# Index scores in column groups, and seven block products for eight over two slabs in the FFN's output projection

## The reference, cut to what matters

```
def swiglu(h, w_up, w_down):                 # w_up 1024 x 5632, w_down 2816 x 1024
    g, u = jnp.split(h @ w_up, 2, axis=-1)
    return (jax.nn.silu(g) * u) @ w_down
...
# in each layer, with mod = silu(c) @ w_ada + b_ada
x = x + 0.5 * mod[:, 2] * rmsnorm(swiglu(h, ffn_w_in[l, 0], ffn_w_out[l, 0]), norm_g[l, 1])
...
# in the mixer's sparse branch: index scores of 4 heads, width 64, then the largest keys
isc = jnp.einsum('bqhd,bkd->bqhk', qib, k_idx).astype(jnp.float32) * (IDX_DIM ** -0.5)
isc = jnp.einsum('bqhk,bqh->bqk', jax.nn.relu(isc), wib.astype(jnp.float32)) * (IDX_HEADS ** -0.5)
...
vals, idx = lax.top_k(isc, topk)
```

## Time and profile before

| | us |
|---|---|
| median of 3 runs | 2609.43 (2607.01 to 2613.8) |
| the profiled execution, its own time | 2608.09 |
| its span in the profile | 2606.2 |
| TensorE busy | 2493.3 (96%) |
| VectorE busy | 1040.1 (40%) |
| ScalarE busy | 566.1 (22%) |
| mean granted clock of TensorE | 0.988 of full |

### The profile page before, as it was taken

The page is one execution under the profiler, slowest core; times in us unless marked ns, Lnnn a source line. Parts: engine busy times, 40 slices in busy tenths (PEclk is TensorE's granted clock), DMA queues, the critical chain, the costliest instruction groups (busy, mean ns, idle before and its releaser), DMA issues.

```text
span 2606.2 us, 40922 instructions
## 1 busy us (share of the span) xinstructions
PE 2493.3 (96%) x17084; PEld 2095.9 (80%) x17084; DVE 1040.1 (40%) x2388; ACT 566.1 (22%) x1262; POOL 63.1 (2%) x100
## 2 busy tenths in 40 slices
PE   7999999999999899999999999999999999999998
PEld 6999997656666589999989999965566665999997
DVE  3455202203676435554016660112066854266501
ACT  3000003114544322000021001120235442310101
POOL 0000000000012100000000000000000120000000
PEclk8999999999999999999999999999999999999998
DMA  8566421542369544665642232225414783323321
GB/s 300 186 226 216 165 89 51 143 136 70 110 224 298 166 148 162 227 225 176 219 142 89 98 120 89 94 67 139 130 61 159 254 283 129 130 73 122 109 89 69
DMA packets 299559, 389.92 MB, mean 150 GB/s; under 512 B 33677, under 2 KB 245385, under 8 KB 299378
## 3 DMA queue, kind: packets, MB, share of 16 engines
q1 hardware_dynamic: 281538, 339.52, 38.9%
q0 software_dynamic: 10752, 38.93, 4.6%
q10 hardware_dynamic: 7088, 8.87, 0.9%
HBM read 377.66 MB, written 9.62 MB: 149 GB/s over the span
## 4 chain that ended last, share of the span: by engine, by line
PE 87%; DMA 6%; DVE 3%; ACT 2%; SPq 1%; issue 1%; ACTq 0%; DVEq 0%; POOL 0%; POOLq 0%
PE PS L665 25%; PE PS L711 13%; PE PS L791 12%; PE PS L845 8%; PE PS L1037 4%; PE PS L592 3%; DMA QR<-w_ada 3%; PE PS L648 3%; PE PS L632 2%; PE PS L745 2%; PE PS L734 2%; PE PS L996 2%; PE PS L1059 2%; PE PS L1051 2%; PE PS L966 1%; PE PS L1006 1%
## 5 line engine op out<-in xcount | busy, mean ns | idle before, releaser
L711 PE MATMUL PS<-BIG,RING 128*128 128x192 f32 x2112 | 345.8, 326 | 0.0
L711 PEld LDWEIGHTS PS<-BIG,RING 128*128 128x128 f32 x2112 | 343.0, 190 | 1.5 <-issue 1.4
L791 PE MATMUL PS<-RING,H 128*128 128x384 f32 (+1 forms) x960 | 307.2, 482 | 0.0
L791 PEld LDWEIGHTS PS<-RING,H 128*128 128x128 f32 x960 | 181.8, 190 | 121.0 <-issue 0.6
L845 PE MATMUL PS<-H,RING 128*128 128x384 f32 x672 | 224.3, 488 | 0.0
L665 PE MATMUL PS<-OT,RING 128*128 128x192 f32 x1216 | 222.5, 326 | 0.0
L665 PE MATMUL PS<-H,RING 128*128 128x192 f32 x1216 | 213.8, 329 | 0.0
L665 PE MATMUL PS<-OT,QR 128*128 128x192 f32 x1216 | 210.0, 326 | 0.0
L665 PEld LDWEIGHTS PS<-H,RING 128*128 128x128 f32 x1216 | 199.0, 191 | 5.6 <-issue 5.4
L665 PEld LDWEIGHTS PS<-OT,RING 128*128 128x128 f32 x1216 | 201.8, 190 | 0.0
L665 PEld LDWEIGHTS PS<-OT,QR 128*128 128x128 f32 x1216 | 199.7, 190 | 0.0
(11 more groups left out here) (242 smaller groups left out, 3122.0 us busy)
## 6 DMA issues: line engine op xcount, KB each, us to landing
RING<-ffn_w_in SPq DMA_DIRECT2D x80, 1024.0 KB, 7.2
QR<-w_ada SPq DMA_DIRECT2D x66, 1024.0 KB, 9.4
RING<-w_in SPq DMA_DIRECT2D x64, 768.0 KB, 6.0
RING<-ffn_w_out SPq DMA_DIRECT2D x32, 768.0 KB, 4.6
RING<-ffn_w_out SPq DMA_DIRECT2D x32, 640.0 KB, 5.9
QKT<-cache_sb_k SPq DMA_DIRECT2D x16, 768.0 KB, 6.1
QR<-cache_sb_v POOLq DMA_DIRECT2D x16, 768.0 KB, 4.9
QKT<-cache_fox_k SPq DMA_DIRECT2D x16, 768.0 KB, 6.1
```

The lines of the kernel that those rows point to most:

```text
L711: mm = pe.matmul(PS[:, m + 2 * g, 0:HALF], w[:, k, m * P:(m + 1) * P], HID[:, half * k2 + k, GROUP[g]], start=(half == 0 and k == 0), stop ...
L791: mm = pe.matmul(PS[:, n % 3, 0:width], H[:, k, tt * P:(tt + 1) * P], w[:, k, :], start=(k == 0), stop=(k == KD - 1))
```

## The change

**Output tiles.** Tiles 0 to 5 of each FFN are made two at a time in seven block products for eight. The blocks: two tiles of outputs (m), two halves of the inner features (contraction steps 0 to 10 and 11 to 21), two column groups of tokens. The 11 steps of a block are taken in two slabs, six and five, and a ring slot holds a slab's steps of both halves. For each slab VectorE makes three sums of weights (`out_weight_sums`, into SO) and one in place; sums of HID (T1 to T4) go to QKT, QBLK and H, as `hidden_sums` during swiglu_in and the rest (T4) at the begin of swiglu_out. Seven banks (3, 4, 5, 6, 0, 1, 2) collect the products over both slabs, and VectorE puts them together into Y. ScalarE copies one product to P1O and then squares and scales Y in SBUF (`scaled_y`). Since QKT is in use, XGATE and XIN are loaded behind the last load of ffn_w_out and not at the second pair. w_ada units write bank 7. QBLK is zeroed in each layer, before the rotations.

**Index scores.** The four pairs of samples go to four column groups of 32, each alone in its columns; QIP shrinks from 4 x 640 to 4 x 128. Gate tiles 6 and 7 go in front of heads 2 and 3, with their copies on ScalarE behind heads 1 and 2, prompt_scores(0) moves behind head 3, all later gate tiles move up by two, and the steps keep seven tiles of nine. FE moves within QR.

```
-GATE_PROMPT = [[6, 7, 8], [9, 10], [11], [12], [13], [14]]
-GATE_STEP = dict(zip((0, 1, 2, 3, 4, 6, 11, 17, 22), range(15, 24)))
+GATE_SCORE = [6, 7]
+GATE_PROMPT = [[8, 9, 10], [11, 12], [13], [14], [15], [16]]
+GATE_STEP = dict(zip((0, 1, 2, 3, 5, 12, 19), range(17, 24)))
...
+KF = NFF // 2
+SLAB = [(0, 6), (6, 5)]
+SEVEN_OUT = 3
...
# SyncE: load_out, and behind the loop over the six slabs
+                if mp < SEVEN_OUT:
+                    j, n = SLAB[half]
+                    d = ring(l, r, 2 * n, 256)
+                    rows = [(d[:, i * n:(i + 1) * n, :], w[:, i * KF + j:i * KF + j + n]) for i in range(2)]
...
+                if f == 0:
+                    ...
+                        sp.dma_start(XGATE[:, k:k + 4, :], ...).then_inc(xslot_full, 16)
+                elif l + 1 < DEPTH:
+                    load_first_in(l + 1, 0)
...
# TensorE: swiglu_out, for mp in range(3), for half in range(2)
+                        if first:
+                            if mp == 0:
+                                pe.wait_ge(gu_free, gu + 24)
+                            else:
+                                pe.wait_ge(p1o_copied, n)
+                        mm = product(3, a11, b11)
+                        if not first:
+                            mm.then_inc(po_ready, 1)
+                        if first and mp:
+                            pe.wait_ge(po_taken, 3 * n - 2)
+                        mm = product(4, a12, b21)
...
+                        pe.wait_ge(so_ready, n * 2 + half + 1)
+                        pe.wait_ge(to_ready, 3 * fn + (1 if first else 3))
+                        if first and mp:
+                            pe.wait_ge(po_taken, 3 * n - 1)
+                        product(5, s1, t1)
...
+                        mm = product(6, a21, t3)
...
+                        mm = product(0, s2, t2)
...
+                        product(1, s4, b22).then_inc(so_free, 1)
+                        if first:
+                            pe.wait_ge(to_ready, 3 * fn + 2)
+                        product(2, a22, t4).then_inc(*((half_used, 1) if first else (y_ready[1], 2)))
                         if l == 0 and a <= ADA_LAST[f]:
-                            ada_in_turn(a)
+                            pe.wait_ge(mod_free, a + 1)
+                            ada_in_turn(a, 7, P)
...
# TensorE: index scores
                     if h >= 2:
                         pe.wait_ge(relu_ready, l * 6 + (h + 1))
+                        gate_tile(GATE_SCORE[h - 2], h - 2, 0)
                     for half in range(2):
                         for bp in range(4):
-                            mm = pe.matmul(PS[:, 4 + 2 * (h % 2) + half, 0:264], QIP[:, h, bp * P:(bp + 1) * P],
-                                           KIT[:, bp, half * 264:(half + 1) * 264], start=(bp == 0), stop=(bp == 3))
+                            mm = pe.matmul(PS[32 * bp:32 * bp + 32, 4 + 2 * (h % 2) + half, 0:264], QIP[:, h, bp, :],
+                                           KIT[:, bp, half * 264:(half + 1) * 264], start=True, stop=True)
                     mm.then_inc(is_ready, 1)
-                    if h == 2:
-                        prompt_scores(0)
-
+                pe.wait_ge(gate_taken, l * 24 + GATE_SCORE[-1] + 1)
+                prompt_scores(0)
...
# VectorE: swiglu_in
+                    if p >= KF + 2 and p % 2 == 1:
+                        hidden_sums(l, f, p - KF - 2, 2)
...
+                    if p == PAIRS - 2:
+                        out_weight_sums(l, f, 0)
...
+            def hidden_sums(l, f, j, n):
+                dve.wait_ge(gu_free, l * 44 + f * 22 + KF + j + n + 3)
+                ...
+                V.tensor_tensor(t1, b12, b11, ALU.subtract).then_inc(vch, 1)
+                V.tensor_tensor(t3, b22, b12, ALU.subtract).then_inc(vch, 1)
+                dve.wait_ge(vch, 2)
+                ins = V.tensor_tensor(t2, b22, t1, ALU.subtract)
...
+            def out_weight_sums(l, f, q):
+                n = l * RINGS + R_OUT[f] + q
+                dve.wait_ge(slot_full[n % 2], 32 * (n // 2 + 1))
+                ...
+                V.tensor_tensor(s1, a21, a22, ALU.add).then_inc(vch, 1)
+                V.tensor_tensor(a21, a11, a21, ALU.subtract).then_inc(vch, 1)
+                dve.wait_ge(vch, 1)
+                V.tensor_tensor(s2, s1, a11, ALU.subtract).then_inc(vch, 1)
+                dve.wait_ge(vch, 3)
+                V.tensor_tensor(s4, a12, s2, ALU.subtract).then_inc(so_ready, 1)
...
# VectorE: swiglu_out, for q in range(6): ada_rows, out_weight_sums(q + 1), ada_columns; behind every second slab
+                    dve.wait_ge(p1o_copied, n + 1)
+                    dve.wait_ge(po_ready, 3 * n + 2)
+                    V.tensor_tensor(out[:, 0:HALF], PS[:, 4, 0:HALF], P1O, ALU.add).then_inc(po_taken, 1)
+                    dve.wait_ge(po_ready, 3 * n + 3)
+                    V.tensor_tensor(U2O, PS[:, 0, 0:HALF], P1O, ALU.add).then_inc(vch, 1)
...
+                    V.tensor_tensor(out[:, 3 * HALF:4 * HALF], PS[:, 5, 0:HALF], U43O[:, GROUP[1]], ALU.add).then_inc(po_taken, 1)
+                    dve.wait_ge(y_ready[1], 8 * b + 2 * mp + 2)
+                    V.tensor_tensor(out[:, HALF:3 * HALF]..., PS[:, 1:3, 0:HALF], U43O..., ALU.add).then_inc(po_taken, 1)
+                    dve.wait_ge(po_taken, 3 * n + 3)
+                    dve.sem_inc(ysum_ready, 1)
...
# VectorE: mixer, behind the first operation on LF
+                link(V.memset(QBLK, 0.0))
```

More of the change, by code:

```diff
@@ L350, in load_out @@
                 w = t["ffn_w_out"][l, f].rearrange("(k p) n -> p k n", p=P)
-                d = ring(l, r, NFF // 2, 256)
-                k0 = half * (NFF // 2)
-                load(l, r, [(d[:, a:b, :], w[:, k0 + a:k0 + b, bass.ds(mp * 256, 256)]) for a, b in ((0, 6), (6, 11))])
+                if mp < SEVEN_OUT:
[3 more added lines that the diff above has]
+                else:
+                    d = ring(l, r, KF, 256)
+                    rows = [(d[:, a:b, :], w[:, half * KF + a:half * KF + b]) for a, b in ((0, 6), (6, KF))]
+                load(l, r, [(x, y[:, :, bass.ds(mp * 256, 256)]) for x, y in rows])
             def by_k(l, r, w, col, width, k=KD):
@@ new lines, in swiglu_out @@
+                        w = ring(l, r, 2 * kn, 256)
+                        a11, a12, a21, a22 = (w[:, i * kn:(i + 1) * kn, m * P:(m + 1) * P] for m in range(2) for i in range(2))
+                        s1, s2, s4 = (x[:, 0:kn * P].rearrange("p (k c) -> p k c", c=P) for x in SO[half])
+                        t1, t2, t3, t4 = (x[:, j:j + kn, :] for x in TO)
+                        b11, b21, b22 = HID[:, j:j + kn, GROUP[0]], HID[:, KF + j:KF + j + kn, GROUP[0]], HID[:, KF + j:KF + j + kn, GROUP[1]]
@@ new lines, in swiglu_out, with product @@
+                        first = half == 0
+                        def product(bank, a, x):
+                            for k in range(kn):
+                                mm = pe.matmul(PS[:, bank, 0:HALF], a[:, k, :], x[:, k, :],
+                                               start=(half == 0 and k == 0), stop=(half == 1 and k == kn - 1))
+                            return mm
+                        if first:
+                            if mp == 0:
+                                pe.wait_ge(gu_free, gu + 24)
+                            else:
+                                pe.wait_ge(p1o_copied, n)
@@ L1647, in swiglu_out @@
                 pending = None
-                for blk in range(6):
-                    if blk % 2 == 1:
-                        scale_y(b, blk - 1)
-                        scale_y(b, blk)
+                fn = 2 * l + f
+                hidden_sums(l, f, KF - 1, 1)
+                for j, n in SLAB:
+                    V.tensor_tensor(TO[3][:, j:j + n, :], HID[:, KF + j:KF + j + n, GROUP[0]], TO[1][:, j:j + n, :],
+                                    ALU.subtract).then_inc(to_ready, 1)
+                for q in range(2 * SEVEN_OUT):
+                    mp, half = divmod(q, 2)
+                    if pending is not None:
+                        ada_rows(pending, P)
+                    if q + 1 < 2 * SEVEN_OUT:
+                        out_weight_sums(l, f, q + 1)
                     if pending is not None:
```

153 lines of the change are left out of this document (100 added, 53 removed).

## The result

The changed kernel takes 2592.13 us (median of 4 runs, 2587.54 to 2594.75), the kernel before beside it 2609.19; the ratio is 0.993, with a 95% interval of 0.991 to 0.9951. So 17 us are gained where 36 were forecast, and 2592.13 lies 2.1 us above the range. The profiled execution took 2593.86 us, its span 2592.0, 14.2 less than before.

What follows compares the result with a forecast made beforehand. TensorE, busy 96% of the span, was taken as the bound, but VectorE's chain in the index stage. Terms: -42.9 + 1.0 + 2.8 + 3.4 = -35.7, giving 2573 us; range 2557 to 2590.

Steps and rivals of the forecast that it cites:

- Seven products: FFN output tiles: 264 matmuls fewer at 0.1625 us each, -42.9 us, with waits for weights and sums costed at 0.
- (b): Seven products partly held up, slab weights or sums 0.5 to 1.2 us late at 24 slabs: 2585 to 2602; chance 0.17.
- (c): Sums 2 us late at every slab, each gap bringing the clock down: 24 x 3.9 = 94, 2666; chance 0.06.
- (d): Column groups of the index scores don't run side by side: 2573 + 14; chance 0.03, inside (b)'s times.
- The moved load: XGATE or XIN load behind the last ffn_w_out load may slow that load: 0.3 us in three places, +1.
- Index stage: New order of heads and gate tiles shifts all behind it by 4.1 us a layer; TensorE's saving of 20 not counted.
- the rule that it names on reading PSUM out: Index scores: once TensorE is four times faster, reading PSUM out may be the limit; 0 instead of -20 us.
- The clock: New 4.2 us gap in the index stage lowers TensorE's clock: +1.9 a layer, +3.4 in all, bounds 0 and 5.
- the four steps' 30.2 us: Steps 4 to 7: 7.7, 9.7, 7.7 and 5.1 us, against 28.7 before, so 1.5 us longer with one tile fewer.
- the list of waits of 2 us and more: Eight TensorE waits looked at in the profile before; after five of them the clock ended at its lower level.
- Steps 8 to 23: Tiles at 12 and 19 replace 11, 17 and 22: 4.2 us less a layer, bounds 2 and 4.6.

Runs made afterwards that it cites:

- e9_filler_index: The changed kernel with five unused matmuls of 128x384 ahead of TensorE's first wait for a relu copy between the index heads; 2581.5 us, ratio 0.9911.
- e3_groups_only: The changed kernel, column groups kept, but with every gate tile at its place of the kernel before; 2564.15 us, ratio 0.9834.

## Why the prediction was right and wrong

**Seven products: right, term and reasons.** 42.9 us were forecast and 4 x 10.72 = 42.9 measured, with no idle time before L730 and no new waits of its w_ada units (18.2 us of idle time before them, as in the L592 group of the earlier trace rows). Rivals (b) and (c), sums or weights late, didn't come about, nor (d): a head takes 1.1 us.

**The moved load: too dear.** 1.0 us was set; the waits of L786 are 10.6 us, and those of the same matmuls before were 10.2, so 0.4.

**Index stage: right.** Of the 7.0 us a layer, 2.0 and 1.5 are the clock by e9_filler_index (1.9 forecast; at the tile itself it is 2.4) and 5.0 and 5.5 the order (4.1). One reading was off: the prediction says that the trace agrees with the rule that it names on reading PSUM out, but its rows have head 0's copy wait for VectorE to have read RL, a buffer in SBUF. That VectorE's chain bounds the stage is what e3_groups_only shows.

**The clock: this term failed.** "+1.9 a layer, times nearly two: +3.4", with 5 as its upper bound, counted the one gap of the index stage. That gap cost 3.5, as forecast. But the clock comes to 17.3 in the profiled execution: 3.5 there, 2 x 4.2 behind the two waits in steps 4 to 7, 2 x 2.1 at the end of the steps, 2 x 0.6 in steps 0 to 3. I had worked out that steps 4 and 6 would leave TensorE waiting for VectorE's copy, had put the wait into the four steps' 30.2 us (29.9 where the clock stays up), and had beside me the list of waits of 2 us and more of which five in eight ended at the lower level; but I didn't hold the new waits of the steps against it. Nor did I ask what the removal of the tile at step 22 would leave TensorE with. Shown by filler are the first two of the four. The third rests on the comparison of kernels with a tile at step 22 (10.1 to 12.3 us from the last scores to the branch in ten layers, 11.3 in the mean) and without one (11.4 to 13.9 in eighteen, 13.3 in the mean). That of steps 0 to 3 was not tested: only the granted clock of 0.72 in the window at 716 us, behind a wait of 1.99 us, speaks for it, and the kernel before has the same wait and stays at 1.00.

**Steps 8 to 23: the value of a tile was mis-sized.** 4.2 us less a layer were forecast for one tile fewer, and steps 8 to 22 got 3.0 us shorter in both layers together. Part of that is the one execution: over all layers with either order the difference is 3.0 us a layer, 86.7 against 89.7. The tile taken away is that of step 22, which lay partly beside waits for masks: the step took 8.2 us with it, and 7.8 and 5.8 without (5.8 in the mean of eighteen layers). So it cost 2.4 us in its step and saved 2.0 behind it, by the clock. How much of the rest is transfers, and how much their spread from run to run, stays open.

The sum as measured: -42.9 + 0.4 + 10.5 (order in the index stage) + 2.4 (order in steps 4 to 7) - 3.0 (steps 8 to 22) + 17.3 (clock) = -15.3, and 14.2 less in the profiled execution. Against the forecast of -35.7 the clock makes up 13.9 us of the miss, steps 8 to 22 5.4 and the order in the index stage 2.3.

## What to carry to other kernels

Work that fills an idle engine has to be issued ahead of the wait that makes the idle time; behind it, wait and work add up, and this case lost 4 to 5 us a layer by that, 1.5 to 2.0 of them through the clock. Before a filler is taken from a place, ask what it covered there: the tiles of steps 4 and 6 stood beside VectorE's rounds, and that of step 22 held up the clock, so each was nearly free where it was. A gap costs only if what stands behind it is waited for: with no tile behind the same gap, the slow head cost nothing. And when a change opens a wait on TensorE, list all of them with the clock's price for each, not only the longest.

## What the runs showed of the hardware

The same 16 records of a gate tile took 5.43 us at a granted clock of 1.00 and 7.83 us behind 4.18 us of idle time, at 0.55 to 0.59, and matmuls whose result nobody reads, put into that idle time, brought it back to 5.43. The Trainium skill (TensorE: Matmul & The Clock Gate, The HAM clock gate) tells of idle stretches that halve the clock, and the trace agrees behind the wait of 4.18 us. What I hadn't expected is how unsteady it is. Two waits of 2.98 us, in the same order of work, left the clock at 1.00 in some layers and brought it to 0.50 in others, and the same four steps took 29.9 to 35.5 us. That such falls move the kernel from one execution to the next is likely but not shown stage by stage: of the changed kernel's four runs the fastest, 2587.54 us, has a mean granted clock of 0.980, the other three, 2590.40 to 2594.75 us, 0.974 to 0.976.
